# Two transformer blocks on one NeuronCore: in-projection tiles in pairs, earlier splits for the down stages, a reordered recurrent chain, and a bias map computed in two parts

## The reference

```
bias = rel_bias[_t5_bucket(dist)]              # dist: query position - key position, 4 heads
logits = einsum(q, k) * scale + bias
merged = g0 * (o_rwkv @ w_r) + g1 * (o_mla @ w_m) + g2 * (o_diff @ w_d)
x = x + merged @ w_o ;  x = x + conv_ffn(rmsnorm(x)) ;  return rmsnorm(x)
```

## Time and profile before

| | |
|---|---|
| median of 3 runs | 2553.18 us (2553.05 to 2558.97) |
| profiled execution | 2550.05 us |
| its span | 2548.7 us |
| mean granted TensorE clock | 0.972 of full speed |
| PE busy | 95% of the span |
| DVE, ACT, POOL busy | 47%, 38%, 17% |
| PE on the chain that ended last | 81% |

### The profile page before, as it was taken

The page is one execution under the profiler, slowest core; times in us unless marked ns, Lnnn a source line. Parts: engine busy times, 40 slices in busy tenths (PEclk is TensorE's granted clock), DMA queues, the critical chain, the costliest instruction groups (busy, mean ns, idle before and its releaser), DMA issues.

```text
span 2548.7 us, 38444 instructions
## 1 busy us (share of the span) xinstructions
PE 2408.7 (95%) x15464; PEld 1979.8 (78%) x15464; DVE 1210.2 (47%) x1797; ACT 970.3 (38%) x1540; POOL 441.2 (17%) x318
## 2 busy tenths in 40 slices
PE   7999999999999999999999989879988899998988
PEld 4777777666667777778888866669987897798988
DVE  4333222545653323243333346566655755676764
ACT  4222212455442222242222244345435324555762
POOL 1000000100000000000000039999994000000000
PEclk9999999899999999999999989999998899999999
DMA  7554455311034444323222241114544221244444
GB/s 281 209 182 176 160 200 184 97 50 50 34 132 168 179 177 164 136 85 115 90 92 84 96 117 67 66 67 158 178 148 143 84 105 55 84 149 149 170 151 141
DMA packets 51943, 329.51 MB, mean 129 GB/s; under 512 B 6480, under 2 KB 7504, under 8 KB 20976
## 3 DMA queue, kind: packets, MB, share of 16 engines
q1 hardware_dynamic: 48608, 318.46, 35.1%
q0 software_dynamic: 3216, 9.36, 1.3%
HBM read 323.99 MB, written 3.80 MB: 129 GB/s over the span
## 4 chain that ended last, share of the span: by engine, by line
PE 81%; DVE 8%; ACT 7%; issue 2%; DMA 2%; SPq 0%; ACTq 0%; DVEq 0%
PE bank L1083 24%; PE bank L1084 22%; PE bank L1085 22%; DVE wlo L539 2%; PE bank L825 2%; PE bank L1658 1%; PE bank L1591 1%; ACT sil L1044 1%; ACT whi L537 1%; PE bank L1680 1%; PE bank L2184 1%; DMA first_ada<-in_stream 1%; ACT u_hi L1047 1%; ACT probs L1628 1%; ACT probs_t L1665 1%
## 5 line engine op out<-in xcount | busy, mean ns | idle before, releaser
L1083 PE MATMUL bank<-u_hi,whi 128*128 128x512 f32 (+1 forms) x2512 | 882.3, 351 | 39.4 <-DVE wlo L539 13.2
L1084 PE MATMUL bank<-u_lo,whi 128*128 128x512 f32 (+1 forms) x2512 | 860.2, 342 | 0.0
L1085 PE MATMUL bank<-u_hi,wlo 128*128 128x512 f32 (+1 forms) x2512 | 858.5, 342 | 0.0
L1083 PEld LDWEIGHTS bank<-u_hi,whi 128*128 128x128 f32 x2512 | 485.8, 193 | 140.9 <-issue 50.6
L539 DVE TENSOR_TENSOR wlo<-raw,whi 128x2048 fp32r<-128x2048 f32 (+2 forms) x213 | 435.1, 2044 | 302.9 <-ACT whi L537 302.6
L1085 PEld LDWEIGHTS bank<-u_hi,wlo 128*128 128x128 f32 x2512 | 486.5, 194 | 53.1
L1084 PEld LDWEIGHTS bank<-u_lo,whi 128*128 128x128 f32 x2512 | 486.9, 194 | 47.8 <-issue 0.2
L537 ACT ACTIVATE whi<-raw 128x2048 fp32r<-128x2048 f32 (+2 forms) x213 | 360.9, 1695 | 171.1 <-PE bank L1085 118.2
L1145 ACT ACTIVATE sil<-bank 128x512 f32<-128x512 f32 (+1 forms) x88 | 47.9, 545 | 619.7 <-PE bank L1085 619.6
L1149 DVE TENSOR_TENSOR prod<-sil,bank 128x512 f32<-128x512 f32 (+1 forms) x88 | 54.7, 621 | 460.0 <-ACT sil L1145 456.9
L1247 POOL TENSOR_SCALAR bucket_step<-distance,bucket_steps 128x384 f32<-128x384 f32 x124 | 251.9, 2031 | 12.6
(11 more groups left out here) (418 smaller groups left out, 2940.2 us busy)
## 6 DMA issues: line engine op xcount, KB each, us to landing
raw<-in_stream SPq DMA_DIRECT2D x231, 1024.0 KB, 4.8
raw<-in_stream SPq DMA_DIRECT2D x80, 704.0 KB, 4.0
first_ada<-in_stream SPq DMA_DIRECT2D x8, 1024.0 KB, 17.0
raw<-in_stream SPq DMA_DIRECT2D x8, 768.0 KB, 4.4
skew<-rpb_rows POOLq DMA_DIRECT2D x8, 336.0 KB, 6.6
nbr_bias<-skew POOLq DMA_DIRECT2D x24, 112.0 KB, 4.0
h<-in_tokens SPq DMA_DIRECT2D x1, 2048.0 KB, 12.0
uq_ukv<-in_small POOLq DMA_DIRECT2D x1, 1536.0 KB, 6.8
```

What stands on the lines that cost most here:

```text
L1083: pe.q.matmul(dst, w[0], x[0], start=start, stop=False)
L1084: pe.q.matmul(dst, w[0], x[1], start=False, stop=False)
L1085: return pe.q.matmul(dst, w[1], x[0], start=False, stop=stop)
```

## The change

It has eight parts. The first two tiles of each in-projection are multiplied together, chunk by chunk (`first_tiles`). In norms of two streams chunks 3 and 6 go the narrow way too. Behind the last group of an up stage the second panel of the down stage is split before that group is evacuated (`ahead`), and the down stage leaves that split out (`early`). The bias map's arithmetic waits for the second panel of the out-projection and stops after 20 of 31 borders; the other 11 are issued after `e1`. Three small loads go from POOL's queue to SP's, behind the second rwkv panel. The first side panel is multiplied in pairs by chunk. In the recurrent chain `angles` is called ahead of the rows' scaling, Sigmoid comes before Tanh, `kk` before the decay's exponential, two reciprocals right after the scan, and some `dense` counts are one higher. The first two differential heads' units get one more quarter each.

```diff
@@ load_rest: the three loads on SP
+            if ph.name == "rwkv_in":
+                second_block()
...
+    def second_block_tables():
+        sp.wait_ge(*hidden_free)
+        sp.dma_start(prow[:, :], ins["pos_row"]).then_inc(s_row_pos, 16)
+        sp.dma_start(wag[:, :], ins["small"][:, SM_WA:SM_N]).then_inc(s_wag, 16)
+        sp.dma_start(tab[:, :], ins["const"][:, CC.at["causal"]:CC.n]).then_inc(s_tab2, 16)
@@ Stream.run, after the last group
+        if ahead:
+            for piece in (0, 1, 2, 3):
+                self.split_piece(after, 1, piece)
         evacuate(Count(m), (g0 + m) % 2, Count(g0 + m), done)
...
-        st.run(name, multiply, evacuate, finish_hidden(n, hidden, h0), early=name != ("up1", 0))
+        st.run(name, multiply, evacuate, finish_hidden(n, hidden, h0), early=name != ("up1", 0), ahead=True)
...
-        st.run(name, multiply, evacuate, ppg=2)
+        st.run(name, multiply, evacuate, ppg=2, early=True)
@@ norm
-            par, slim = x % 2, x < narrow
+            par, slim = x % 2, x < narrow or (streams == 2 and x % 3 == 0)
@@ bias_map
-        pool.after((s_pos, 32))
+        pool.after((s_pos, 32), (st.s_pe, PHASE[("out", L1 - 1)].first + 2))
...
-        for b, start in enumerate(bucket_starts()):
+        return bias_steps(z, 0, 20)
+
+    def bias_steps(z, lo, hi):
+
+        for b in range(lo, hi):
+            start = bucket_starts()[b]
             for hh in range(DH):
@@ in-projection
-                if i < 2:
-                    pe.after(ready[kc])
...
+        def first_tiles():
+
+            n = [q_cols(kind) for kind, _ in IN_TILES[0:2]]
+            places = [next_bank() for _ in n]
+            pe.q.wait_ge(st.s_lo, in_first + 1)
+            for kc in range(KC):
+                pe.after(ready[kc])
+                first = three(places[0][1][:, 0:n[0]], tile_of(in_first % 2, kc), chunk_of(u, kc, 0, n[0]), kc == 0, kc == KC - 1)
+                if kc == KC - 1:
+                    half_done = pe.do(first)
+                second = three(places[1][1][:, 0:n[1]], tile_of(in_first % 2, KC + kc), chunk_of(u, kc, 0, n[1]),
+                               kc == 0, kc == KC - 1)
+            second.then_inc(st.s_pe, 1)
...
@@ side_quarter, first side panel
-            if n == 0 and b == 0:
+        if n == 0:
+            for kc in range(2 * q, 2 * q + 2):
                 pe.after(ready[kc])
+                for b in range(2):
+                    r = three(side_target(0, b), tile_of(slot, b * KC + kc), chunk_of(u, kc, 0, S), kc == 0, kc == KC - 1)
@@ recurrent chain
+    trig_done = angles()
     for i in range(4):
         dense(2)
...
-    trig_done = angles()
     dc = act.do(act.q.activation(flat4(dec[:, :, :]), flat4(dec[:, :, :]), ACT.Exp, scale=-float(np.exp(-0.5))))
...
+    dve.after(scanned, z1)
+    pinv = [dve.do(dve.q.reciprocal(by_chunk(dec[:, :, :])[:, c, :, :], Pb[:, c, :, 1:CH + 1])) for c in range(2)]
     dense(3)
...
-    dense(4)
+    dense(5)
...
         if c == 1:
-            dense(2)
+            dense(3)
...
-    dense(3)
+    dense(4)
@@ after the first level of the inverse
     e1 = dve.do(dve.q.tensor_tensor(v16(TT[:, :, :]), ident_rows, v16(Mm), ALU.subtract))
+    pool.after(e1)
+    map_ready = bias_steps(map_ready, 20, NBUCKET - 1)
     dense(2)
@@ differential heads
-        dense(1 + i % 2)
+        dense(1 + i % 2 + (i < 2))
```

More of the change, by code:

```diff
@@ L595, in split_lo, with run @@
             r.then_inc(self.s_lo, 1)
-    def run(self, name, multiply, evacuate, finish=None, ppg=1, loop=True, second=None, third=None, early=False):
+    def run(self, name, multiply, evacuate, finish=None, ppg=1, loop=True, second=None, third=None, early=False, ahead=False):
         ph = PHASE[name]
@@ L1530, in program @@
         def program():
-            for i, tile in enumerate(IN_TILES):
+            yield from first_tiles()
+            for i in range(2, len(IN_TILES)):
                 yield from in_tile(i)
@@ L1980, in build @@
     act.after(mixed[12], mixed[13])
+    m1 = act.do(act.q.activation(mix[:, 13, :], mix[:, 13, :], ACT.Sigmoid))
     m0 = act.do(act.q.activation(mix[0:64, 12, :], mix[0:64, 12, :], ACT.Tanh))
-    m1 = act.do(act.q.activation(mix[:, 13, :], mix[:, 13, :], ACT.Sigmoid))
     dense(2)
@@ L2751, in up_hidden @@
                             ALU.subtract).then_inc(s_hl, 1)
-    st.run("up_2", pair_multiply, up_evac, second=up_product, third=up_hidden, early=True)
+    st.run("up_2", pair_multiply, up_evac, second=up_product, third=up_hidden, early=True, ahead=True)
     hidden_count[0] += FC
```

58 lines of the change are left out of this document (29 added, 29 removed).

## The result

The changed kernel takes 2617.8 us (median, 2616.83 to 2618.67), the kernel before 2553.11 us beside it: a ratio of 1.025 (1.0232 to 1.0269), 2.5% slower. The forecast was 2593 us, with a range up to 2614. The sign and the stall were right, and the time lies outside the range. The profiled execution took 2618.67 us, its span is 2617.4.

What follows compares the result with a forecast made beforehand. Bound taken: PE's stream of matmuls, busy 2408.7 of 2548.7 us, with many small stalls. Profiled 2550.05 + 80 loss - 38.5 gains = 2591.5; with the median above that execution, forecast 2593 us, range 2568 to 2614.

Steps and rivals of the forecast that it cites:

- The map: Bias map in two parts: DVE's wait for the late 44 pairs leaves PE idle, 78 us lost, 68 to 83.
- The clock behind it: After the map's stall PE returns at its lower clock: 2 us lost, between 0 and 3.
- The first tiles in pairs: In-projections of both layers, first two tiles multiplied together: 11 us gained, 6 to 13.
- The bank wait of the forecast: In-projection: tile 2 waits for tile 0's bank, 0.8 us with the semaphores.
- Narrow chunks: Norm chunks 3 and 6 the narrow way: 1.5 us gained, between -3 and 5.
- The second down panel: Narrow down stages, second panel split ahead: 5 us gained, 3 to 8; nothing in wide stages.
- The map off layer 1's attention: Layer 1's attention, DVE no longer slowed by the map: 6 us gained, 2 to 10.
- The map beside the second block: Map now runs beside the start of the second block: 2 us lost, 0 to 5.
- The chain: Recurrent chain: angles and reciprocals moved, three more quarters fill PE's waits: 13 us gained, 8 to 18.
- The pairs of the first side panel: First side panel multiplied in pairs, ending near 1940 instead of 1944.22: 4 us gained, 2 to 5.
- The three loads: Three loads from POOL's queue to SP's: cost nothing, 4.8 us at most without cover.
- Rival (b): Gains fail: DVE paces norms, side-panel splits bound the chain, extra quarters wait for weights; 2618 us, chance 0.14.

Runs made afterwards that it cites:

- e2: Kernel before with only the bias map's new gate and two parts, its three small loads still on POOL's queue: 2661.0 us, one run.
- e6: Whole change with the bias map as before and all five extra quarters of side panels taken back: 2531.4 us (0.9913).
- e10: Whole change, map in two parts, with only the five extra quarters taken back: 2612.3 us (1.023).
- e12: Whole change with old quarter counts, the map late but in one part, DVE's wait for it just ahead of the difference heads: 2532.5 us (0.9916).
- e8: Whole change with the old map, and angles, reciprocals and quarter counts as before: 2532.5 us (0.9918).
- e9: Whole change with the old map, the recurrent chain's three extra quarters taken back, the difference heads' two kept: 2532.7 us (0.992).
- e4: Whole change with the old map and angles() back at its old place behind the g products: 2541.7 us, one run.
- e11: Whole change with old map and old quarters, angles split: DVE's part behind Sigmoid and Tanh, ACT's sines behind the g products: 2527.9 us (0.9901).
- e14: Whole change with old map and old quarters, except one extra quarter kept behind the decayed keys: 2538.7 us (0.9949).
- e5: Kernel before with only the first block's edits (tiles in pairs, narrow chunks, second down panel ahead); map, loads, second block as before: 2536.9 us (0.9938).
- e3: Changed kernel, map in two parts, DVE's wait for it and the additions moved just ahead of the difference heads: 2567.5 us, one run.
- e13: Whole change with old map and old quarters, except one extra quarter kept behind the products for b: 2539.4 us (0.9943).

## Why the prediction was wrong

**The map: right.** Stall 78 us forecast, 76.7 on DVE and 78.6 on PE measured, in e2 as well (78.60). The clock behind it is 0.80 over 16 us, some 3 us, the upper end of the 0 to 3 given. What the Trainium skill's rule gave as an end, 83 us (SBUF — State Buffer, "Who interferes with whom": the ports that DVE and GpSimd share are an exclusive lock, held for the whole instruction in the case of DVE's two-port modes), the trace doesn't show. In the 55.9 us before its wait DVE held 5 splits of 11.9 us and 5 masks of 6.7 us, 18.6 us in all (one split more than before, by the shifted quarters). Shut out for all of that, POOL would have done (55.9 - 18.6) / 2.77 = 13.5 pairs, and it did 16.1. Two splits show where the rest went:

```profile
2026.06 2.28 DVE L541 TENSOR_TENSOR wlo<-raw,whi 128x2048 fp32r<-128x2048 f32 x1
2026.25 4.59 POOL L1255 TENSOR_SCALAR bucket_step<-distance,bucket_steps 128x384 f32<-128x384 f32 x1 [53.74 <-DVE inverse_t L2217]
...
2078.10 1.57 POOL L1255 TENSOR_SCALAR bucket_step<-distance,bucket_steps 128x384 f32<-128x384 f32 x1
2078.70 2.29 DVE L541 TENSOR_TENSOR wlo<-raw,whi 128x2048 fp32r<-128x2048 f32 x1 [6.00 <-ACT whi L539]
```

The POOL instruction that starts inside a split takes 3.0 us longer, about what the split and the mask right behind it still last. The one under way when a split starts keeps its 1.57 us. Eight POOL instructions start inside such DVE work, and together they are 11.6 us longer, which is all that the 16.1 pairs lost.

**The first tiles in pairs: right, a little large.** 11 us forecast. The 16 steps of layer 0 take 13.2 us (457.64 to 470.80) instead of 19.85, as forecast, but the stretch gains less than these 6.7 us. Layer 0's stretch falls from 269.1 (270.8 in e2, the same code there) to 264.9, the mean of 18 profiles of the new code; layer 1's with the old map from 212.2 to 208.0, the mean of 13. Together some 9, narrow chunks included. The bank wait of the forecast stands in the profile after as 0.57 us at the first step of tile 2.

**Narrow chunks: nothing**, forecast 1.5, inside its bounds. The second feed-forward of layer 0, between two such norms, takes 407.3 us before and 407.1 after. In the in-projections they were not run apart from the pairs.

**The second down panel: right, on the low side.** 5 us forecast, measured 3.4 in layer 1 (209.5 to 206.1, the mean of 13 with the old map) and 3.7 at the end (209.7 to 206.0). In the last stage 2.37 us stay of 4.92.

**The map off layer 1's attention: undersized.** 6 us forecast, 9.7 measured (208.0 with the old map, 196.7 to 199.4 and on the mean 198.3 in the five profiles with the late one), inside its bounds of 2 to 10.

**The map beside the second block: the second wrong term.** 2 us forecast, "0 to -5". Against e6, e10 has 1.3 us more to the scan and 2.4 more to the first inverse, and the second feed-forward of layer 1 is 1.3 us longer on the mean of the five profiles with the late map: some 5, the end of its bounds. In e12, where POOL works through the whole chain, it is 2.1 + 6.2 + 1.5. I had priced POOL beside DVE as a mean over a long stretch and not by the instructions that stand there, one of which, the scan, pays 2.35 us alone.

**The chain: the step that failed.** "The angles leave the path of the 6.1 us wait, which goes; ... three more quarters of side panels fill PE where it waits for 3.08 us and 3.35 us", 13 us. The runs put nothing in its place for the order of angles and reciprocals (e8 and e6 are alike) and a loss of about 10 us for these three quarters (e9). Two mistakes:
- I moved the angles' issue past DVE's and PE's work and forgot ACT's queue. ACT's absolute value waits for a chain of eight DVE instructions. Wherever the block is called whole, ACT stands 4.4 to 8.0 us in front of it, and what is queued there (a panel's evacuation and the next split) is what PE needs next. e4 and e11 show it: moved back, the block changes the time by 1 us; split in two, it leaves 0.78 and 1.30 us where waits of 7.5 and 7.1 us stood.
- I priced the extra quarters by the gap they fill. They filled it (e14: 4.13 to 2.69 us), but each shifts the border between two panels, and with it the place of a 2.3 us split in DVE's order in everything that follows. Behind the levels it then stands ahead of the clearing of the state. All five cost 11.3 us with the old map, and 5.5 in the changed kernel, where the rest hides in the stall.

The pairs of the first side panel were priced rightly: 3.7 against 4. The three loads were not: priced at nothing, they keep a wait of 3.14 us (e5) off the chain with the old map and one of 33 us (e2) with the late one.

**The sum again**, by the stretches of the table: layer 0 -3.5, layer 1 -13.8 and -2.3, chain to the first inverse +7.5, levels with the stall +78.9, to the heads +4.1, the rest of the block +1.0, the end -4.1. That is +67.8 of the 68.6 us between the two profiled executions. The chain's line was to be -13 - 4 + 2 = -15. The forecast's own sum is a little off as well: with the median's 3.1 us it gives 2594.7 and not 2593, which decides nothing.

**Rival (b)** gave 2618, the time that came. Its mechanism was half right: the splits of side panels are the chain's bound. But the norms did not become DVE's, the first block's gains stood, and the quarters did worse than wait for weights. That its number fits is luck in part: the first block's gains, which it denied, and the chain's loss, which is larger than it said, cancel. The 27.1 us of waits that it was built on were those of the whole span; between the block's constants and the first inverse they were 5.2. The range should have let the chain's term go below zero.

## What to carry to other kernels

A block that runs over two engines has two places in the order, one on each queue; move the part that produces early and the part that consumes late, and look on both queues at what is then behind it. Filler was not neutral here: its own setup (here a split for every fourth quarter) moves with the count, so after changing a count look at where the setup falls ahead of something small that PE waits for, and put that small thing earlier. A wait for slow background work belongs just ahead of the first use: e3 gained 50 us by it.

## What was not expected of the hardware

- Beside a busy POOL DVE's scan of 16 x (128x64) takes 5.38 us instead of 3.03, and two reciprocals of 128x256 3.36 and 3.37. POOL's own pairs stay at 2.81 us during the scan. With DVE's long two-input instructions it is the other way round: the split keeps 2.28 us and the POOL instruction that starts inside it stands.
- Sigmoid ahead of Tanh saves a table load: the kernel before has one for each (at 1953.75 and 1955.48), the changed kernel loads once (1.28 us at 1936.13) and then runs both. This is as the Trainium skill has it (ScalarE activation tables: per-element evaluation and per-set limits, "What a function is on this engine"): two functions of one set need no switch.
- A shorter first block made the second one longer: its code is the same in the kernel before and in e5, but e5 takes 46.5 us to the scan and not 41.6, since a load queued on POOL behind the map doesn't come earlier with it.
- One stretch of one profile can differ by 3 us where code and waits are the same. In the heads e14 took 198.3 us and e13 201.8, with a granted clock of 0.97 and 0.96.
